# First input passed channels-first, small vectors and narrow weights as one load each, first loads in alternating pieces

## The reference: what is computed

```python
def reference(x, attn_norm, w_in, b_forget, ..., final_norm):
    h = x
    for layer in range(DEPTH):
        a = rmsnorm(h, attn_norm[layer])
        h = h + hybrid_mixer(a, w_in[layer], b_forget[layer], ..., w_out[layer])
        m = rmsnorm(h, ffn_norm[layer])
        i = layer // 2
        if layer % 2 == 0:
            h = h + swiglu(m, dense_w_gate[i], dense_w_up[i], dense_w_down[i])
        else:
            h = h + moe_swiglu(m, router_w[i], moe_w_gate[i], moe_w_up[i], moe_w_down[i])
    return rmsnorm(h, final_norm)
```

## Time and profile before

| what | value |
|---|---|
| median of 3 executions | 2266.33 us (2265.36 to 2267.01) |
| the profiled execution's own time | 2267.55 us |
| its span, first to last instruction | 2265.8 us |
| PE busy | 2223.3 us, 98% of the span |
| DVE / ACT / POOL busy | 1565.7 / 1237.9 / 375.3 us |
| moved by the transfers | 515.40 MB, mean 227 GB/s |

### The profile page before, as it was taken

The page is one execution under the profiler, slowest core; times in us unless marked ns, Lnnn a source line. Parts: engine busy times, 40 slices in busy tenths (PEclk is TensorE's granted clock), DMA queues, the critical chain, the costliest instruction groups (busy, mean ns, idle before and its releaser), DMA issues.

```text
span 2265.8 us, 29186 instructions
## 1 busy us (share of the span) xinstructions
PE 2223.3 (98%) x10255; PEld 1826.5 (81%) x10255; DVE 1565.7 (69%) x1725; ACT 1237.9 (55%) x1524; POOL 375.3 (17%) x180
## 2 busy tenths in 40 slices
PE   7999999999999999999999999999999999999997
PEld 6888888888888888888877888888877888888875
DVE  4466686666655666665564466686679999999998
ACT  5445454454444444444435445454457887878875
POOL 1111211222222222222222111221220000000000
PEclk9999999999999999999999999999999999999999
DMA  7454545555555555555655464545589999999996
GB/s 246 149 191 158 185 153 189 182 175 191 184 193 195 185 191 195 188 184 189 200 167 168 149 197 152 186 158 196 194 311 342 360 367 366 365 381 366 367 362 224
DMA packets 264461, 515.40 MB, mean 227 GB/s; under 512 B 15528, under 2 KB 19740, under 8 KB 263324
## 3 DMA queue, kind: packets, MB, share of 16 engines
q1 hardware_dynamic: 260880, 502.51, 64.8%
q0 software_dynamic: 3312, 11.90, 1.7%
q10 hardware_dynamic: 200, 0.05, 0.0%
HBM read 508.81 MB, written 13.65 MB: 231 GB/s over the span
## 4 chain that ended last, share of the span: by engine, by line
PE 78%; DVE 10%; issue 5%; ACT 4%; DMA 3%; ACTq 0%; DVEq 0%; POOLq 0%; SPq 0%
PE acc L1565 20%; PE acc L1567 20%; PE acc L1566 20%; PE acc L1859 4%; PE acc L1861 4%; PE acc L1860 4%; DVE w_lo L982 3%; DMA scr<-tokens_dram,slot_token 3%; ACT w_hi L643 2%; PE X L1840 1%; PE X L1673 1%; DVE sm L987 1%; DVE nat L1125 1%; PE X L1593 0%; DVE eg L1469 0%
## 5 line engine op out<-in xcount | busy, mean ns | idle before, releaser
L643 ACT ACTIVATE w_hi<-raw 128x1024 fp32r<-128x1024 f32 x744 | 778.6, 1058 | 608.6 <-PE acc L1567 558.0
L982 DVE TENSOR_TENSOR w_lo<-raw,w_hi 128x1024 fp32r<-128x1024 f32 x606 | 758.4, 1271 | 477.3 <-ACT w_hi L643 474.9
L1565 PE MATMUL acc<-w_hi,a_hi 128*128 128x512 f32 x1632 | 643.7, 394 | 4.0 <-DVE w_lo L982 2.4
L1567 PE MATMUL acc<-w_hi,a_lo 128*128 128x512 f32 x1632 | 636.4, 390 | 0.0
L1566 PE MATMUL acc<-w_lo,a_hi 128*128 128x512 f32 x1632 | 635.8, 390 | 0.0
L576 POOL TENSOR_TENSOR w_lo<-raw,w_hi 128x1024 fp32r<-128x1024 f32 x138 | 337.8, 2448 | 1304.9 <-ACT w_hi L643 1005.3
L1565 PEld LDWEIGHTS acc<-w_hi,a_hi 128*128 128x128 f32 x1632 | 306.8, 188 | 67.7 <-DVE w_lo L982 3.8
L1567 PEld LDWEIGHTS acc<-w_hi,a_lo 128*128 128x128 f32 x1632 | 306.4, 188 | 64.9
L1566 PEld LDWEIGHTS acc<-w_lo,a_hi 128*128 128x128 f32 x1632 | 306.9, 188 | 61.3
L1859 PE MATMUL acc<-w_hi,a_hi 128*128 128x512 f32 x752 | 302.4, 402 | 4.2 <-DVE w_lo L982 4.1
L1861 PE MATMUL acc<-w_hi,a_lo 128*128 128x512 f32 x752 | 294.1, 391 | 0.0
(11 more groups left out here) (236 smaller groups left out, 1492.4 us busy)
## 6 DMA issues: line engine op xcount, KB each, us to landing
raw<-in_w_in SPq DMA_DIRECT2D x112, 1024.0 KB, 5.0
raw<-in_moe_w_gate SPq DMA_DIRECT2D x64, 1024.0 KB, 12.9
more_raw<-in_moe_w_up SPq DMA_DIRECT2D x64, 1024.0 KB, 12.7
raw<-in_dense_w_gate SPq DMA_DIRECT2D x44, 1024.0 KB, 5.2
raw<-in_dense_w_up SPq DMA_DIRECT2D x44, 1024.0 KB, 5.1
raw<-in_dense_w_down SPq DMA_DIRECT2D x44, 1024.0 KB, 5.1
raw<-in_w_out SPq DMA_DIRECT2D x32, 1024.0 KB, 5.2
raw<-in_moe_w_down SPq DMA_DIRECT2D x32, 1024.0 KB, 12.3
```

The lines of the kernel that those rows point to most:

```text
L643: nc.scalar.activation(w_hi[:, slot], raw_tile(tile)[1][:, u % TILE_UNITS], ACT.Copy)\
L982: nc.vector.tensor_tensor(w_lo[:, slot], raw_tile(u // TILE_UNITS)[1][:, u % TILE_UNITS], w_hi[:, slot].bitcast(F32), ALU.subtract).then_i ...
L1565: nc.tensor.matmul(dst, hi, w_hi[:, slot, c], start=first and c == 0, stop=False)
L1567: ins = nc.tensor.matmul(dst, lo, w_hi[:, slot, c], start=False, stop=last and c == UNIT_CHUNKS - 1)
```

## The change

Inputs: the host passes `x` a second time as `x_t`, already channels-first (partition, chunk of 128 channels, token); all gain vectors and the forget gates' biases as one array `gains`, channel on the partition; and the narrow weights of both layers and the router as one array `thin_w` in the layout of their tile. `x` itself is still loaded, in two pieces of 128 tokens.

Code: PE's transposes of the first input and of the gains are gone, and in their place stand `WARM` = 10 products of a tile of ones with itself, whose results nobody reads. `first_input_hi` and `first_input_lo` make `a_hi` and `a_lo` from `x_cols` (the landed `x_t`, in the memory of `nat`), two chunks ahead of each unit's weights. SP's first loads alternate between pieces of `x_t` (2, 2, 4 and 8 chunks) and weights, tile 0 in two halves, with no wait among them. The squares move from units 2 and 4 to 4 and 5, the root from unit 5 to 6, the split of the narrow weights from units 6 and 7 to unit 3.

```diff
+XT_PIECES = (0, 2), (2, 4), (4, 8), (8, 16)
+WARM = 10
...
-    SQUARE_FIRST, SQUARED_FIRST = {2: 0, 4: 1}, 5
+    SQUARE_FIRST, SQUARED_FIRST = {4: 0, 5: 1}, 6
+    THIN_AT = 3
...
+        x_cols = nat[:].rearrange("p a b n -> p (a b n)").rearrange("p (k n) -> p k n", k=CH)
...
+        bf = gain[0:HEADS, NROWS:NROWS + DEPTH]
...
-            def load_x(c):
-                sp_.dma_start(h[:, :, c * COLS:(c + 1) * COLS],
-                              x[0, :, c * COLS:(c + 1) * COLS].rearrange("(b p) n -> p b n", p=P)).then_inc(x_in[c], 16)
-
-            load_x(0)
+            def load_x(b):
+                sp_.dma_start(h[:, b, :], x[0, b * P:(b + 1) * P, :]).then_inc(x_in[b], 16)
+
+            def load_x_cols(n):
+                k0, k1 = XT_PIECES[n]
+                sp_.dma_start(x_cols[:, k0:k1, :], x_t[:, k0:k1, :]).then_inc(xt_in[n], 16)
+
             for layer in range(DEPTH):
                 tile = layer_start[layer] // TILE_UNITS
                 for j, (_, _, col) in enumerate(jobs):
                     if layer == 0 and j == 0:
-                        load(0, w_in[0, 0:COLS, col:col + COLS])
+                        for half, landed in enumerate((first_in, loaded[0])):
+                            load_x_cols(half)
+                            r = half * UNIT_CHUNKS * P
+                            sp_.dma_start(raw[:, 0, half], w_in[0, r:r + UNIT_CHUNKS * P, col:col + COLS]
+                                          .rearrange("(c p) n -> p c n", p=P)).then_inc(landed, 16)
+                        load_x_cols(2)
+                        load(1, w_in[0, COLS:2 * COLS, col:col + COLS])
+                        load_x_cols(3)
+                        load(2, w_in[0, 2 * COLS:3 * COLS, col:col + COLS])
+                        load_x(0)
+                        load(3, w_in[0, 3 * COLS:4 * COLS, col:col + COLS])
+                        sp_.dma_start(thin.rearrange("p t c n -> p (t c n)"), thin_w).then_inc(thin_in, 16)
                         load_x(1)
-
-                        sp_.wait_ge(small_in, 16 * N_SMALL)
-                        for t in range(1, CH // GC):
-                            load(t, w_in[0, t * COLS:(t + 1) * COLS, col:col + COLS])
-                            if t + 1 < NCOL:
-                                load_x(t + 1)
-                        for l in range(DEPTH):
-                            sp_.dma_start(thin[:, l], w_in[l].rearrange("(c p) n -> p c n", p=P)[:, :, 3 * W + 4 * W:])\
-                               .then_inc(thin_in, 16)
-                        sp_.dma_start(thin[:, 2], router_w[0].rearrange("(c p) n -> p c n", p=P)).then_inc(thin_in, 16)
...
+                if u == 0:
+                    act.wait_ge(first_in, 16)
...
+            def first_input_hi(u):
+
+                if u == 0:
+                    act.wait_ge(small_in, 16)
+                for n, (k0, k1) in enumerate(XT_PIECES):
+                    if k0 == UNIT_CHUNKS * u:
+                        act.wait_ge(xt_in[n], 16)
+                for k in range(UNIT_CHUNKS * u, UNIT_CHUNKS * u + UNIT_CHUNKS):
+                    nc.scalar.activation(a_hi[:, k, :], x_cols[:, k, :], ACT.Copy,
+                                         scale=gain[:, NG_ATT + k:NG_ATT + k + 1]).then_inc(a_hi_ready, 1)
...
-            for src, at, n in ((attn_norm, NG_ATT, CH), (ffn_norm, NG_FFN, CH), (sb_out_norm, NG_HEAD, HEADS),
-                               (fox_out_norm, NG_HEAD + DEPTH * HEADS, HEADS)):
-                act.dma_start(rows[at:at + DEPTH * n, :], src.rearrange("l (c p) -> (l c) p", p=P)).then_inc(small_in, 16)
-            act.dma_start(rows[NG_QK:NG_QK + 2, :], fox_q_norm[:, :]).then_inc(small_in, 16)
-            act.dma_start(rows[NG_QK + 2:NG_QK + 4, :], fox_k_norm[:, :]).then_inc(small_in, 16)
-            for l in range(DEPTH):
-                act.dma_start(bf[:, l:l + 1], b_forget[l].rearrange("(n o) -> n o", o=1)).then_inc(small_in, 16)
-
+            act.dma_start(gain[:, 0:NROWS + DEPTH], gains).then_inc(small_in, 16)
...
                     for u in range(LEAD):
+                        first_input_hi(u)
                         split_hi(u)
-                        if u == 0:
-                            act.wait_ge(gain_ready, 1)
-                        input_hi(0, u)
                 for u in range(ATT_UNITS):
+                    if L == 0 and u + LEAD < JOB_UNITS:
+                        first_input_hi(u + LEAD)
                     split_hi(U0 + u + LEAD)
-                    at_start(2 * L, u)
+                    if L:
...
-                        if b == 0:
-                            for c in range(NCOL):
-                                act.wait_ge(x_in[c], 16)
-                        else:
+                        act.wait_ge(x_in[b], 16)
+                        if b:
...
-                    if layer == 0 and u == JOB_UNITS - 2:
-                        act.wait_ge(thin_in, 16 * (DEPTH + 1))
+                    if layer == 0 and u == THIN_AT:
+                        act.wait_ge(thin_in, 16)
...
+            def first_input_lo(u):
+
+                if u == 0:
+                    dve.wait_ge(small_in, 16)
+                for k in range(UNIT_CHUNKS * u, UNIT_CHUNKS * u + UNIT_CHUNKS):
+                    dve.wait_ge(a_hi_ready, k + 1)
+                    nc.vector.scalar_tensor_tensor(
+                        out=a_lo[:, k, :], in0=x_cols[:, k, :], scalar=gain[:, NG_ATT + k:NG_ATT + k + 1],
+                        in1=a_hi[:, k, :].bitcast(F32), op0=ALU.mult, op1=ALU.subtract).then_inc(a_ready, 1)
...
+            pe.wait_ge(consts, 1)
+            for n in range(WARM):
+                nc.tensor.matmul(X[:, n % 4, 0:P], ones[:], ones[:], start=True, stop=True)
             pe.wait_ge(consts, N_CONSTS)
-            turn_input(0, 0)
-
-            pe.wait_ge(small_in, 16 * N_SMALL)
-            nc.tensor.transpose(X[:, 3, 0:NROWS], rows[0:NROWS, :], ident[0:NROWS, 0:NROWS]).then_inc(gain_ps, 1)
-            pe.wait_ge(gain_ready, 1)
-            turn_input(0, 1)
-            turn_input(0, 2)
...
-                            if ju == 1:
+                            if ju == 1 and L:
...
+    wide = laid["w_in"].shape[2] // COLS * COLS
+    thin = _np.concatenate([laid["w_in"][:, :, wide:], laid["router_w"]])
+    laid["thin_w"] = thin.reshape(thin.shape[0], -1, P, thin.shape[2]).transpose(2, 0, 1, 3).reshape(P, -1)
+    laid["x_t"] = laid["x"][0].T.reshape(-1, P, BLOCKS * P).transpose(1, 0, 2)
+    norms = [laid[n].reshape(-1, P) for n in ("attn_norm", "ffn_norm", "sb_out_norm", "fox_out_norm", "fox_q_norm", "fox_k_norm")]
+    bias = laid["b_forget"].T
+    laid["gains"] = _np.concatenate([_np.concatenate(norms).T, _np.pad(bias, ((0, P - bias.shape[0]), (0, 0)))], axis=1)
```

More of the change, by code:

```diff
@@ L66, in lin, with trunk @@
     return const if i is None else i * per + const
-def trunk(nc, x, attn_norm, w_in, b_forget, fox_q_norm, fox_k_norm, sb_out_norm, fox_out_norm, w_out,
-          ffn_norm, dense_w_gate, dense_w_up, dense_w_down, router_w, moe_w_gate, moe_w_up, moe_w_down,
+def trunk(nc, x, x_t, gains, w_in, thin_w, w_out,
+          ffn_norm, dense_w_gate, dense_w_up, dense_w_down, moe_w_gate, moe_w_up, moe_w_down,
           final_norm, out):
@@ L74, in trunk @@
     CH = D // P
-    HEADS = sb_out_norm.shape[1] // P
-    W = sb_out_norm.shape[1]
-    EXPERTS = router_w.shape[2]
+    W = w_in.shape[2] // 7 // P * P
+    HEADS = W // P
+    EXPERTS = moe_w_gate.shape[1]
     F_EXP = moe_w_gate.shape[3]
@@ L200, in trunk @@
         thin = eg[:, 0, 0:3 * P].rearrange("p (t c n) -> p t c n", t=3, c=CH)
-        rows = eg[:, 1, 0:P]
         NG_ATT, NG_FFN, NG_HEAD, NG_QK = 0, 2 * CH, 4 * CH, 4 * CH + 4 * HEADS
@@ L271, in trunk @@
         free = [sem(f"free{s}") for s in range(2)]
-        x_in = [sem(f"x_in{c}") for c in range(NCOL)]
+        x_in = [sem(f"x_in{b}") for b in range(BLOCKS)]
+        xt_in = [sem(f"xt_in{n}") for n in range(len(XT_PIECES))]
+        first_in = sem("first_in")
         small_in = sem("small_in")
@@ L403, in h_ready @@
         def h_ready(eng, n, c):
-            if n == 0:
-                eng.wait_ge(x_in[c], 16)
-            elif n == 2:
+            if n == 2:
                 eng.wait_ge(free[1 - c % 2], att_uses[1] - 1 + c // 2)
@@ L636, in split_hi @@
                 tile = u // TILE_UNITS
-                if u % TILE_UNITS == 0:
+                if u % TILE_UNITS == 0 and u:
+                    tile_loaded(act, tile, per, i)
+                if u == 0:
+                    act.wait_ge(first_in, 16)
+                if u == 1:
                     tile_loaded(act, tile, per, i)
@@ L692, in norm_guess @@
                 rsqrt_guess(rr, ss, 2, 1.0 / D, ss_ready)
+            def first_input_hi(u):
[7 more added lines that the diff above has]
+                                         scale=gain[:, NG_ATT + k:NG_ATT + k + 1]).then_inc(a_hi_ready, 1)
             def input_hi(n, quarter):
-                act.wait_ge(xnT_ps, 4 * n + quarter + 1)
```

(35 more changed lines are left out.)

5 lines of the change are left out of this document (removed).

## The result

| | before | after |
|---|---|---|
| median of 5 runs | 2266.03 us (2265.36 to 2267.01) | 2254.07 us (2253.8 to 2254.87) |
| the profiled execution | 2267.55 us | 2254.87 us |
| its span | 2265.8 us | 2253.1 us |

The ratio is 0.9948, with a 95% interval of 0.9936 to 0.9961: 12.0 us faster, where 8.5 were forecast. The direction was right.

A forecast was written before the change was run, and what follows sets the result against it. The start was taken as bound by the small loads, then by `x`. Unit 8 at 9.2 + 21.8 + 1.55 + 0 = 32.55 in place of 41.11 saves 8.55 us: 2257.8 from the median 2266.33, range 2255.2 to 2261.2.

The forecast's parts named there:

- Part 1: Program start: half tile and gains at 6.1, then 0.8 for `a_hi`, 1.06 and 1.22 for splits; unit 0 at 9.2 us.
- Part 2: PE's clock: the products of ones change nothing; unit 0 starts at 1.2 GHz for 3.3 us, costing 1.55; bounds 0 and 3.1.
- Part 3: Feeding units 2 to 8: weight tiles land in time, PE never waits, 1.4 us or more to spare; unit 7 tightest.
- Part 4: Moved work: squares on ACT hidden by 0.6 us before unit 9; removing the three narrow loads gains nothing PE waited for.
- the mark: Start of narrow products behind unit 8, 43.83 us before; what unit 8 gains, the end should gain; forecast near 35.3.
- The sum: Unit 8 starts at 9.2 + 21.8 + 1.55 + 0 = 32.55 in place of 41.11, 8.55 us less.
- its own bound: Best case: unit 0 at 8.0 with a high clock, tile 4 holds PE, unit 8 near 30.6, saving 10.5 us.
- the 0.6 for the spread of executions: Allowance in us for differences between executions, used with rival 4 to set the range 2255.2 to 2261.2.
- Rival 1: Weight loads each pay for themselves, 1.65 us: tile 4 lands 14.9 later, 2271.2 us, slower; 3 in 100.
- Rival 2: PE's clock stays low through the first job: 9.4 us later, 2275.7 us, slower; 2 in 100.
- Rival 3: Loads slower in this mix, 0.30 MB per us: tile 4 at 35.1, saving 3.7, 2262.6 us; 5 in 100.
- rival 4: Gains land last, at 8.9: unit 0 at 12.0, unit 8 at 35.4, saving 5.7, 2260.6 us; 8 in 100.

The follow-up runs named there:

- without pieces: After with `x_t` as one load ahead of the weights and tile 0 whole, against unchanged after: 2261.83 us, ratio to before 0.9985.
- the run with the narrow loads: After with the three old narrow loads in place of the one load of narrow weights: 2259.79 us, ratio to before 0.9977.
- the third chip: Unchanged after measured again beside before on another chip: 2254.61 us against 2264.34, ratio 0.9954.
- the old order of arrays: After's program unchanged, its arrays declared in before's order with the new ones last: 2255.10 us, ratio to before 0.9957.
- the third comparison: Unchanged after beside before on one chip, with kernels that change one part at a time: after 2256.36 us, before 2265.05, ratio 0.9965.
- the smaller pieces: After with tile 1 also in two halves and the third piece of `x_t` cut in two: 2255.85 us, ratio to before 0.996.

## Why the prediction was wrong

**Part 1, unit 0 at 9.2.** It came at 8.48. The half tile was right: forecast at 6.1, ACT began on it at 6.02. The step that failed is the landing of the gains: I took 6.1, between bounds of 4.6 and 7.8 worked out from the old loads' packets, and they landed at 4.41, outside the bounds. With them early the 0.8 us for `a_hi` lie ahead of the half tile and leave the path. 6.02 and two splits, with the hand-overs between the engines, make 8.48. Eight small loads that a queue worked off beside others said little about one load issued at 0.83 ahead of most of them. Nor is 4.41 a constant of that load: with `x_t` in one piece it came at 9.05. The half tile, too, came earlier in the other profiles of after, at 5.41 to 5.77 by ACT's rows, and unit 0 at 7.87 to 8.23.

**Part 2, the clock at 1.55.** It cost nothing. The size was right for the start at 1.2 GHz without the burst (1.4 us; without pieces it was 2.1), but the step "they change nothing" failed, and by a price: I put a product of ones at the duration of a transpose, also 128 columns, and so the burst at 2.4 us. In the trace ten products are twenty records and take 4.64 us. After them and 1.37 us of idling the first products ran at 2.4 GHz; after the same burst and 6.88 us of idling they ran at 1.2. The burst differs from the transposes' bursts of about 2 us in its length and in the idling behind it, and no run separates the two. The bound of 0 held this case.

**Part 3, no waits.** The landings were forecast at 12.2, 17.6, 23.0 and 28.8 and came at 11.99, 17.18, 22.40 and 28.11. Unit 2 was to be ready at 14.5 and started at 14.46. What failed is "no wait, with 1.4 us or more to spare", because PE came sooner: 0.45 before unit 2, and 0.34 before unit 3, whose weights POOL splits, a place that I had not named (I looked at unit 7, which did not wait). The errors of parts 1 and 2 are together 2.3 us, 0.8 of them went into these waits, some 0.2 into small steps, and 1.25 remain: unit 8 at 31.30 in place of 32.55. Tile 4's landing at 28.11 and 2.3 for the splits set a floor near 30.4, which after has nearly reached.

**Part 4, hidden.** It held. Behind unit 8 no wait stands on PE in the time line up to 60 us, with the squares at 25.52 and 29.07 on ACT. Its remark that the narrow loads would need tile 4's time in the new queue is what the run with the narrow loads showed, 4.8 us at the mark.

**The sum and the range.** The start gave 9.8 where the sum had 8.55, and in this pair of profiles its own bound, a saving of 10.5, was not passed. On the third chip the marks, 33.65 against 44.27 and 44.16, are 10.5 to 10.6 apart: about 0.4 because before stays at the low clock longer there (its last slow product starts at 20.04 and 19.88, in the first profile at 18.90), the rest because after is earlier. The 41.11 and the 3.3 us that I built on were one execution's. The other part of the miss, about 2 us, is not in the start, and it is what carried the time out of the range: the term that failed is the 0.6 for the spread of executions. In four comparisons, the last three on three chips, the two programs differed by 12.0, 9.2 (with the old order of arrays), 8.7 and 9.7 us in the medians; before was at 2266.03, 2264.29, 2265.05 and 2264.34, after at 2254.07, 2255.10, 2256.36 and 2254.61. The last four are 2.3 us apart, and the saving was counted from one median of before, 2266.33 of three executions, which is above all four. Against the 0.6, single runs of before in the third comparison lie between 2263.42 and 2268.2. Whether the runs of before in the first comparison had the gather's stall more often stays open, since only one of them is profiled. Open too is the 1 us and more by which the medians fall short of the mark in most rows. In the profiles most of it lies in the stretch behind the dense mixer, 108.7 to 108.9 us in all six profiles whose mark is before 35 us, and 107.5 to 108.6 in the eight others. That the earlier start brings it about was not tested.

**The rivals.** Rival 1 had each load pay its own fixed time. Between 5 and 8 us, when loads of 0.26 and 0.52 MB arrived, 414 GB/s moved, and 388 to 402 in five other profiles with the same queue. The Trainium skill, "DMA: Bandwidth & Descriptors", section "Bandwidth", asks for "≥1 MiB for ≥75% of peak"; the trace does not agree for loads that are queued one behind the other. Some price is there all the same: in the one profile of the smaller pieces about 0.4 us was lost for each load more, where the rival had 1.65. Rival 2 did not come, since the clock was high from the first product on; where it was low at first, it had risen by the eighth product (no burst) and the eleventh (no pieces). Rival 3 (0.30 MB per us) and rival 4 (gains at 8.9) are excluded by the landings in after; the remark against rival 3, that all new rows are of 1.5 KB or more, had overlooked the gains' rows of 408 bytes. Without pieces rival 4's landing did come, 9.05, and cost nothing, because the weights came later still.

## What to carry to other kernels

At the start of a program lay out the landing time of every byte by the rate of the whole queue: here that gave each of four tiles within 0.7 us, and it is a floor that no gain elsewhere on the path passes, as the burst of ones shows (1.4 us better, 0 at the end). The smaller pieces moved the floor itself, 0.8 us the wrong way. A part that costs nothing where its neighbours are slow may cost once they are fast: the narrow loads were hidden in before and worth 3.4 us in after. And for a forecast to half a per cent of a long program, the spread between chips and executions (here 1.7 us between the medians of before, 2.3 between those of after) belongs in the range beside the terms of the sum.

## What the runs showed of the hardware

Two things that I had not expected. DVE's four `a_lo`, read from SBUF, took 3.90 us where two take 0.88 elsewhere, 2.1 more than four at that price, in a stretch in which POOL split a tile (time lines of DVE and POOL, of after):

```profile
10.25 0.88 DVE L1047 SCALAR_TENSOR_TENSOR a_lo<-nat,gain,a_hi 128x256 fp32r<-128x256 f32 x2
...
14.23 3.90 DVE L1047 SCALAR_TENSOR_TENSOR a_lo<-nat,gain,a_hi 128x256 fp32r<-128x256 f32 x4
```

```profile
15.06 2.39 POOL L579 TENSOR_TENSOR w_lo<-raw,w_hi 128x1024 fp32r<-128x1024 f32 x1 [11.16 <-ACT w_hi L650]
```

It is one of the four that is long: it starts at 15.23, behind POOL's start, and takes 2.50 in place of 0.48, until 17.73, just behind POOL's end at 17.45. Five other profiles of the same order show 3.86 to 3.92. The Trainium skill, "SBUF — State Buffer", section "Who interferes with whom", says that a DVE instruction with two inputs in SBUF and a GpSimd instruction that reads SBUF contend for a shared read interface; the trace agrees. Before the change `a_lo` was read from PE's banks and not from SBUF, but DVE's `w_lo`, with two inputs in SBUF, was long beside POOL's too: 1.61 at 22.50 and 2.07 at 45.18, in place of 1.22. PE did not wait for it here.

And one load of 128 short rows, issued by ACT at 0.83, was seen at 4.41, while 16 engines were busy with SP's queue (280 GB/s between 2.5 and 4.5 us). The same load, issued at the same time, was seen at 9.05 when SP's first load was 2.1 MB in packets of 16 KB, with about as many packets of the one as of the other moving in the same time (97 and 98 between 3 and 7 us). When a small load lands beside a full queue depended here on the packets that stood beside it.
